# The weight-block sums of an FFN's seven-product units, moved from VectorE to GpSimd

## What is computed

```
def swiglu(h, w_in, w_out):
    gate, up = jnp.split(h @ w_in, 2, axis=-1)
    return (jax.nn.silu(gate) * up) @ w_out
...
x = x + 0.5 * swiglu(rms_norm(x, ffn1_norm[layer]), ffn1_w_in[layer], ffn1_w_out[layer])
```

## Time and profile before

| | |
|---|---|
| median of 3 runs | 2288.98 us (2287.26 to 2289.0) |
| profiled execution, span from first to last instruction | 2285.9 us |
| PE busy, share of the span | 2249.8 us, 98% |
| DVE busy | 1633.5 us, 71% |
| ACT busy | 1049.8 us, 46% |
| POOL busy | 302.4 us, 13% |
| mean granted TensorE clock | 0.996 |

### The profile page before, as it was taken

The page is one execution under the profiler, slowest core; times in us unless marked ns, Lnnn a source line. Parts: engine busy times, 40 slices in busy tenths (PEclk is TensorE's granted clock), DMA queues, the critical chain, the costliest instruction groups (busy, mean ns, idle before and its releaser), DMA issues.

```text
span 2285.9 us, 45730 instructions
## 1 busy us (share of the span) xinstructions
PE 2249.8 (98%) x18915; PEld 2198.7 (96%) x18915; DVE 1633.5 (71%) x2712; ACT 1049.8 (46%) x1949; POOL 302.4 (13%) x257
## 2 busy tenths in 40 slices
PE   9999999999999999999999999999999999999998
PEld 8999999988989999999999999999988899999998
DVE  7876776557575977767877776689755657777674
ACT  5544444333323544444554444454444544444443
POOL 2100002000051100001200000144033632000001
PEclk9999999999999999999999999999999999999999
DMA  4222323322202233222222232322310012222321
GB/s 135 93 93 97 103 92 110 98 81 83 90 10 93 75 101 103 93 93 93 93 93 93 96 105 87 114 74 75 93 52 2 30 31 91 93 93 93 98 97 68
DMA packets 175052, 194.82 MB, mean 85 GB/s; under 512 B 4826, under 2 KB 155870, under 8 KB 174841
## 3 DMA queue, kind: packets, MB, share of 16 engines
q1 hardware_dynamic: 161902, 181.64, 24.3%
q10 hardware_dynamic: 12306, 8.18, 1.3%
q0 software_dynamic: 640, 2.10, 0.3%
HBM read 185.80 MB, written 6.10 MB: 84 GB/s over the span
## 4 chain that ended last, share of the span: by engine, by line
PE 85%; DVE 8%; ACT 2%; issue 2%; POOL 1%; DMA 1%; ACTq 0%; SPq 0%; DVEq 0%; POOLq 0%
PE ps L892 33%; PE ps L793 29%; PE ps L666 12%; DVE cacc L2419 2%; DVE wl L651 1%; PE ps L3320 1%; DVE pre L2408 1%; ACT cacc L2488 1%; DMA xnat<-x_prompt 1%; PE ps L1681 1%; PE ps L3165 0%; POOL dBl L2996 0%; PE ps L2152 0%; PE ps L3150 0%; PE ps L3200 0%
## 5 line engine op out<-in xcount | busy, mean ns | idle before, releaser
L892 PE MATMUL ps<-bop,wh 128*128 128x272 f32 x4032 | 761.0, 288 | 0.0
L892 PEld LDWEIGHTS ps<-bop,wh 128*128 128x128 f32 x4032 | 633.0, 188 | 0.0
L892 PE MATMUL ps<-bop,wl 128*128 128x272 f32 x2016 | 582.2, 289 | 0.0
L784 DVE TENSOR_TENSOR wl<-raw,wh 128x512 fp32r<-128x512 f32 (+1 forms) x456 | 317.5, 708 | 266.8 <-ACT wh L778 262.1
L892 PEld LDWEIGHTS ps<-bop,wl 128*128 128x128 f32 x2016 | 378.8, 188 | 0.0
L778 ACT ACTIVATE wh<-raw 128x512 fp32r<-128x512 f32 (+1 forms) x456 | 265.3, 611 | 217.2 <-PE ps L793 177.4
L793 PE MATMUL ps<-hl,wh 128*128 128x288 f32 (+1 forms) x1408 | 290.4, 287 | 0.0
L793 PE MATMUL ps<-hh,wl 128*128 128x288 f32 (+1 forms) x1408 | 289.5, 287 | 0.0
L793 PE MATMUL ps<-hh,wh 128*128 128x288 f32 (+1 forms) x1408 | 289.1, 286 | 0.0
L666 PE MATMUL ps<-xh,wh 128*128 128x288 f32 (+1 forms) x1056 | 224.7, 294 | 2.1 <-DVE wl L651 2.1
L778 ACT ACTIVATE wh<-wsum 128x512 fp32r<-128x512 f32 x256 | 159.6, 627 | 132.8 <-DVE wsum L1038 86.6
(11 more groups left out here) (490 smaller groups left out, 3586.5 us busy)
## 6 DMA issues: line engine op xcount, KB each, us to landing
raw<-ffn_w_in SPq DMA_DIRECT2D x88, 1024.0 KB, 5.0
raw<-ffn_w_out SPq DMA_DIRECT2D x32, 1024.0 KB, 5.1
raw<-odd_w_in SPq DMA_DIRECT2D x16, 1024.0 KB, 5.7
raw<-even_w_in SPq DMA_DIRECT2D x14, 1024.0 KB, 5.0
raw<-ffn_w_out SPq DMA_DIRECT2D x16, 768.0 KB, 4.2
raw<-even_w_out SPq DMA_DIRECT2D x4, 1024.0 KB, 5.0
raw<-odd_w_out SPq DMA_DIRECT2D x4, 1024.0 KB, 4.9
xnat<-x_prompt SPq DMA_DIRECT2D x2, 1024.0 KB, 11.9
```

Of the source, the lines that this page charges most:

```text
L784: nc.vector.tensor_tensor(lo[:, 0:nk, :], op_source(u, i), hi[:, 0:nk, :].bitcast(F32), ALU.subtract).then_inc(op_lo.sem, 1)
L892: ins = nc.tensor.matmul(ps[:, bank, 0:TH], w[:, k, :], bop[:, r, k, :], start=i in S_OPEN and k == 0 and a == 0, stop=k == KH - 1 and a = ...
```

## The change

GpSimd makes the four sums of 16 of the 18 seven units of each FFN (64 of 72 units, 256 instructions). The first two seven units of each FFN keep their sums on VectorE. GpSimd's program gets the sums of an FFN as a block of their own, behind the gate products of the FFN's start and ahead of the next layer's sums of squares. For each unit it waits for the load, then for the place in `wsum`: for an FFN's third and fourth seven units until the last plain product is over (until then the normed input lies there), for later ones until VectorE has split the last sum of the unit two before. The sums have a new semaphore, `sum_pool`; ScalarE waits on it in place of `sum_made`. The sums' operands and order stay the same, and so does all else on VectorE.

```
+    SUM_TERMS = (((1, 0), (1, 1), ALU.add), (None, (0, 0), ALU.subtract), ((0, 1), None, ALU.subtract), ((0, 0), (1, 0), ALU.subtract))
+
+    def block_sums_pool(pool, u):
+
+        slot, out = u.raw % 2, sums_of(u)
+        pool.wait_ge(raw_loaded[slot].sem, raw_loaded[slot].at(8 * (u.raw - slot) + 16))
+        if u.seven - first_seven[u.f] < 4:
+            pool.wait_ge(op_used.sem, op_used.at(ffns[u.f][3].op + 4))
+        else:
+            pool.wait_ge(op_lo.sem, op_lo.at(sevens[u.seven - 2].op + 5))
+        for k, (a, b, alu) in enumerate(SUM_TERMS):
+            if a is None or b is None:
+                pool.wait_ge(sum_pool.sem, sum_pool.at(sums_before(u) + k))
+            left = out[:, k - 1, :, :] if a is None else block_raw(u, *a)
+            right = out[:, k - 1, :, :] if b is None else block_raw(u, *b)
+            nc.gpsimd.tensor_tensor(out[:, k, :, :], left, right, alu).then_inc(sum_pool.sem, 1)
+
+    def ffn_sums_pool(pool, f):
+        for u in ffns[f]:
+            if u.kind == "seven" and not early_block(u):
+                block_sums_pool(pool, u)
...
     def weight_sum_dve(dve, u, k):
 
-        if u.kind != "seven":
+        if u.kind != "seven" or not early_block(u):
             return
...
         if u.kind == "seven" and i in S_SUMS:
-            act.wait_ge(sum_made.sem, sum_made.at(4 * u.seven + S_SUMS[i] + 1))
+            sum_wait(act, u, S_SUMS[i] + 1)
...
         ffn_lead_pool(pool, 0, 0)
+        ffn_sums_pool(pool, 0)
         feed_pool(pool, 1)
```

More of the change, by code:

```diff
@@ L406, in build @@
     sum_made = sig("sum_made")
+    sum_pool = sig("sum_pool")
     bank_copied = sig("bank_copied")
@@ L746, in block_nk, with early_block, sums_before, sum_wait @@
         return LAST_TILES - KH if u.kind == "last" and last_blocks(u)[i][1] else KH
+    def early_block(u):
+        return u.seven - first_seven[u.f] < 2
+    def sums_before(u):
+        return 4 * (2 * u.f + u.seven - first_seven[u.f] if early_block(u) else u.seven - 2 * (u.f + 1))
+    def sum_wait(eng, u, count):
+        made = sum_made if early_block(u) else sum_pool
+        eng.wait_ge(made.sem, made.at(sums_before(u) + count))
     def sums_of(u):
@@ L1031, in weight_sum_dve @@
+    def ffn_sums_pool(pool, f):
+        for u in ffns[f]:
+            if u.kind == "seven" and not early_block(u):
+                block_sums_pool(pool, u)
     def weight_sum_dve(dve, u, k):
-        if u.kind != "seven":
+        if u.kind != "seven" or not early_block(u):
             return
-        s, slot, out = u.seven, u.raw % 2, sums_of(u)
+        out = sums_of(u)
         if k == 0:
[L1037 to L1046, removed]
@@ L1048, in lead_product @@
+            dve.wait_ge(raw_loaded[u.raw % 2].sem, raw_loaded[u.raw % 2].at(8 * (u.raw - u.raw % 2) + 16))
+        a, b, alu = SUM_TERMS[k]
+        if a is None or b is None:
+            dve.wait_ge(sum_made.sem, sum_made.at(sums_before(u) + k))
+        left = out[:, k - 1, :, :] if a is None else block_raw(u, *a)
+        right = out[:, k - 1, :, :] if b is None else block_raw(u, *b)
+        nc.vector.tensor_tensor(out[:, k, :, :], left, right, alu).then_inc(sum_made.sem, 1)
     def lead_product(dve, u, c):
@@ L3538, in _ @@
         ffn_lead_pool(pool, 1, 2)
+        ffn_sums_pool(pool, 1)
         feed_pool(pool, 3)
         ffn_lead_pool(pool, 2, 3)
+        ffn_sums_pool(pool, 2)
         feed_pool(pool, 4)
@@ L3544, in _ @@
         ffn_lead_pool(pool, 3, 5)
+        ffn_sums_pool(pool, 3)
         feed_pool(pool, 6)
```

## The result

The changed kernel takes 2296.61 us in the median of 5 runs (2295.51 to 2297.82), beside 2288.68 us for the kernel before on the same chip (2287.26 to 2289.0): 7.9 us more, ratio 1.0036 with a 95% interval of 1.0023 to 1.0048. The forecast was 2297.0 us, and its case, a stall in the first mid unit of each FFN, is what happened. Lines have moved: `x_update` is now L1248, the low split L797, the products of mid units L806, of seven units L905, `hidden_lo` L969; GpSimd's sums are L1059.

A forecast was written before the change was run, and what follows sets the result against it. TensorE's products bound the kernel, so VectorE's relief gains nothing. Span 2285.9 + 4 x 2.0 = 8.0 us gives 2293.9; plus 3.1 to the median, 2297.0 us. Range 2286.5 to 2309, the forecast's own 2294 to 2303.

The forecast's parts named there:

- its case: First mid unit of each FFN: TensorE stands 2.0 us ahead of the third tile, 8.0 us in all; chance 0.48.
- VectorE's relief: 256 sum instructions leave VectorE, 175 us of its busy time; off TensorE's path worth 0.
- the margin of 0.3 us: First mid unit of an FFN: x_update 0 ends at 99.53, TensorE loads tile 2's first weights at 99.85.
- The size: First mid unit of each FFN: 2.0 us lost, taken between 2.3 and 1.6; four FFNs make 8.0 us.
- its walk with turns: First mid unit: four sums hold VectorE 3.8 us; less 1.2 saved and 0.3 margin, TensorE stands 2.3 us.
- the middle: First mid unit: 2.0 us, taken between 2.3 (turns) and 1.6 (VectorE keeps the access through back-to-back work).
- the price of a turn: GpSimd's turn at the shared SBUF access costs a VectorE instruction with two SBUF operands about 1.05 us at 512 columns.
- The choice between taking turns and GpSimd waiting: First mid unit: alternating turns lose 2.3 us; GpSimd waiting for VectorE's PSUM reads loses 1.6.
- the 5.27 us product of the earlier trace: GpSimd product begun at 764.31; VectorE's others went ahead until one read PSUM at 768.27; by it a sum takes 6.4 us.
- Busy time: VectorE's busy time falls by less than 175 us, because held instructions count as busy.
- The margins of later units: Other 28 mid units: x_update 0 and 1 still end 0.6 and 0.4 us before tiles 2 and 3 load; no loss.
- the case of all mid units: Rival: a late split costs 28 later mid units 0.35 us each, 10 us on top of 8, about 2307; chance 0.17.

The follow-up runs named there:

- the two kernels that share out the third unit: Changed kernel with each FFN's third seven-product unit's sums back on VectorE: 2287.89 us; with only that unit's sums on GpSimd: 2296.91 us.
- the kernel with both updates moved: Changed kernel with, in each FFN's first mid unit, x_update 0 before the last split and x_update 1 behind the next unit's first split: 2289.8 us.
- the run beside additions: Kernel before, VectorE making all sums, plus four unread chained GpSimd additions of 128x512 in each FFN's third unit: 2302.16 us, ratio 1.0059.

## Why the prediction was right

**VectorE's relief is worth nothing.** Shown by the run with 240 sums on GpSimd and no change of time, and by TensorE being busy for all 33.07 us of a later pair before and after.

**The place.** Ahead of tile 2 of the first mid unit, once in each FFN, was forecast from the margin of 0.3 us; waits (1.7 to 2.3 us, forecast 1.5 to 2.5), chain and the two kernels that share out the third unit agree.

**The size.** 2.0 us an FFN was forecast, as a middle between 2.3 (each sum gets its turn) and 1.6 (GpSimd waits for VectorE's PSUM reads). The second to fourth FFN lost 2.0 each, but not as a mixture of the two: each sum got its turn. The second FFN, GpSimd's first sum and then VectorE:

```profile
799.23 1.30 POOL L1059 TENSOR_TENSOR wsum<-raw 128x512 f32<-128x512 f32 x1 [23.70 <-DMA raw<-ffn_w_in]
...
799.76 3.10 DVE L969 TENSOR_TENSOR hl<-sq,hh 128x544 fp32r<-128x544 f32 x2 [1.01 <-ACT hh L964]
...
803.25 1.31 DVE L797 TENSOR_TENSOR wl<-raw,wh 128x512 fp32r<-128x512 f32 x1
804.48 1.52 DVE L1280 TENSOR_TENSOR sq<-u3c,m5c 128x272 f32<-128x272 f32 x1
```

The held instructions are the forecast ones: the two L969 take 3.10 us where 1.36 stand in the earlier trace rows, a split 1.31 for 0.69, a combination 1.52 for 0.43. That is 1.74 + 0.62 + 1.09 = 3.45 us, where the prediction had 3.8; less 1.2 and 0.3 it leaves 1.95. The missing part is the first hold: sum 0 had begun 0.5 us before the first L969 came, so the two L969 lost 1.74 and not 2.05. By its walk with turns, which is what happened, the prediction gives 2.3; that the middle hit 2.0 is luck. In the first FFN the same load took 6.3 us to land (issued 85.69, first sum at 92.08), not 5.0, so the L969 were over and the holds fell on the next four, 3.9 us in all; less 1.5 that is 2.4, and the gap was 2.3. The 1.05 us taken as the price of a turn is 1.09 in the trace.

**Who has the access.** The choice between taking turns and GpSimd waiting came out for turns in this stretch. Both kinds occur, though: elsewhere in the changed kernel one sum took 3.33 us while VectorE worked back to back on instructions with two SBUF operands, as the 5.27 us product of the earlier trace rows did:

```profile
104.47 3.33 POOL L1059 TENSOR_TENSOR wsum<-raw 128x512 f32<-128x512 f32 x1 [6.20 <-DMA raw<-ffn_w_in]
...
104.77 1.28 DVE L797 TENSOR_TENSOR wl<-wsum,wh 128x512 fp32r<-128x512 f32 x2
105.97 0.68 DVE L797 TENSOR_TENSOR wl<-raw,wh 128x512 fp32r<-128x512 f32 x1
```

Which of two waiting instructions goes first was not settled. The rule of the Trainium skill (SBUF — State Buffer, "Who interferes with whom") that the first to start has the access for its whole instruction fits the alternating rows here, with 1.09 us a turn, and not those of 3.33 and 5.27.

**Busy time** was forecast to fall by less than 175 us because held instructions count. It did not fall but rose by 37: the reason given is right, its size was not worked out. At 3.3 us held a unit, the figure that the prediction had for a later pair, it could have been: 64 x 3.3 = 211, more than 175.

**The margins of later units** were forecast at 0.6 and 0.4 us. They were 0.35 and 0.25 in the pair above, smaller but enough: in the changed kernel no later pair is more than 0.11 us longer than before. The pair of 33.67 us in the kernel with both updates moved shows how near the case of all mid units was: there the weights took 6.4 us to land, not 5.0, and the sums met the work ahead of `x_update` 0.

**Not foreseen:** the clock behind the first FFN's gap, some 1.7 us of the profiled execution. With it the span is 2295.9 where 2293.9 was forecast; whether other executions had such a stretch, no trace shows.

## What to carry to other kernels

Moving element-wise work to an idle GpSimd isn't free for VectorE: count what GpSimd reads from SBUF at the same time, 0.4 us a turn with one operand of 128x512 here and 0.84 to 1.09 with two, and compare the sum with the margin of whatever VectorE delivers just in time. Find that margin unit by unit in the timeline; here 4 units of 64 made the whole loss and the other 60 had room, though only 0.25 us of it in the pair looked at. A wait that is moved out of the way leaves the delay in the queue, so look up who is late next before pricing the repair.

## What the runs showed of the hardware that was not expected

VectorE was held by GpSimd's copies at 0.4 us a turn, less than half of what the additions cost, and not at all by its memsets. In four kernels TensorE had gaps of 1.7 to 2.7 us ahead of tile 2, sixteen in all. Behind fourteen of them the granted clock stayed at 1.00, but it fell to 0.50 for some 3 us behind one gap of the changed kernel and one of the run beside additions (second FFN, 37.0 us for the pair); what decides it, these runs don't tell.
